# Sorted experts with a two-part operand, and a reordered end of the stick-breaking mixer

## What is computed

```python
def moe_swiglu(h, w_router, wg, wu, wd):          # layer 1 of the first block
    logits = (xt @ w_router).astype(jnp.float32)
    top_v, top_i = lax.top_k(logits, TOP_K)       # 2 of 8 experts for each token
    gates = jax.nn.softmax(top_v, axis=-1)
...
    for e in range(N_EXPERTS):                    # wg, wu: 1024x3584, wd: 3584x1024
        y = y + gate[:, e:e + 1] * swiglu(xt, wg[e], wu[e], wd[e])

def stick_breaking_attention(q, k, v):            # 8 heads, in both layers of the second block
    z = jnp.einsum('bqhd,bshd->bhqs', qb, k) * scale
    log_beta = jax.nn.log_sigmoid(z)
    log_1m = jnp.where(strict, jax.nn.log_sigmoid(-z), 0.0)
    after = lax.cumsum(log_1m, axis=3, reverse=True) - log_1m
    a = jnp.where(strict, jnp.exp(log_beta + after), 0.0)
    return jnp.einsum('bhqs,bshd->bqhd', a, v)
```

## Time and profile before

| | us |
|---|---|
| median of 3 runs | 2488.77 (2488.15 to 2489.57) |
| profiled execution, its own time | 2488.49 |
| its span, first to last instruction | 2486.8 |
| PE busy in the span | 2458.5 |
| DVE busy | 2083.3 |
| ACT busy | 1586.6 |

### The profile page before, as it was taken

The page is one execution under the profiler, slowest core; times in us unless marked ns, Lnnn a source line. Parts: engine busy times, 40 slices in busy tenths (PEclk is TensorE's granted clock), DMA queues, the critical chain, the costliest instruction groups (busy, mean ns, idle before and its releaser), DMA issues.

```text
span 2486.8 us, 44150 instructions
## 1 busy us (share of the span) xinstructions
PE 2458.5 (99%) x17270; PEld 2248.2 (90%) x17270; DVE 2083.3 (84%) x2832; ACT 1586.6 (64%) x2312; POOL 172.0 (7%) x244
## 2 busy tenths in 40 slices
PE   9999999999999999999999999999999999999999
PEld 9999998999999999999998899998899899988998
DVE  5688857999999999999999799786898798786665
ACT  5644556888888888888887644557544544566543
POOL 2111021000000000000000111010111011010000
PEclk9999999999999999999999999999999999999999
DMA  7698545999999999999999688433688587432642
GB/s 295 230 360 318 197 167 205 394 363 378 365 381 365 381 365 379 368 376 369 375 367 393 231 303 321 176 128 128 234 317 295 217 325 288 160 128 77 220 178 77
DMA packets 136637, 696.21 MB, mean 280 GB/s; under 512 B 16528, under 2 KB 16656, under 8 KB 87728
## 3 DMA queue, kind: packets, MB, share of 16 engines
q1 hardware_dynamic: 109872, 598.79, 64.5%
q0 software_dynamic: 23424, 88.16, 9.2%
q10 hardware_dynamic: 3136, 6.43, 0.7%
HBM read 683.28 MB, written 13.24 MB: 280 GB/s over the span
## 4 chain that ended last, share of the span: by engine, by line
PE 89%; DVE 6%; ACT 3%; issue 1%; POOL 0%; DVEq 0%; ACTq 0%; POOLq 0%
PE ps L2390 16%; PE ps L1985 15%; PE ps L1986 15%; PE ps L1987 15%; PE ps L2552 12%; PE ps L2392 8%; DVE w_parts L1705 1%; DVE w_parts L1325 1%; PE ps L2522 1%; PE ps L2014 1%; ACT w_parts L1113 1%; DVE a_parts L1713 1%; PE ps L2010 1%; PE ps L2221 0%; DVE xT L1347 0%
## 5 line engine op out<-in xcount | busy, mean ns | idle before, releaser
L2390 PE MATMUL ps<-a_parts,w_parts 128*128 128x512 f32 x1760 | 618.8, 393 | 1.6 <-DVE a_parts L1290 1.3
L1705 DVE TENSOR_TENSOR w_parts<-ring,w_parts 128x1024 fp32r<-128x1024 f32 x448 | 548.3, 1224 | 53.6 <-ACT w_parts L1113 51.7
L1985 PE MATMUL ps<-w_parts 128*112 128x256 f32 x1792 | 515.5, 288 | 0.0
L1987 PE MATMUL ps<-w_parts 128*112 128x256 f32 x1792 | 498.6, 278 | 0.0
L1986 PE MATMUL ps<-w_parts 128*112 128x256 f32 x1792 | 498.5, 278 | 0.0
L2392 PE MATMUL ps<-a_parts,w_parts 128*128 128x256 f32 x1760 | 492.5, 280 | 0.0
L1113 ACT ACTIVATE w_parts<-ring 128x1024 fp32r<-128x1024 f32 x448 | 472.0, 1054 | 0.0
L2390 PEld LDWEIGHTS ps<-a_parts,w_parts 128*128 128x128 f32 x1760 | 329.8, 187 | 75.7 <-issue 3.6
L2392 PEld LDWEIGHTS ps<-a_parts,w_parts 128*128 128x128 f32 x1760 | 332.3, 189 | 0.0
L1985 PEld LDWEIGHTS ps<-w_parts 128*112 128x112 f32 x1792 | 312.9, 175 | 11.8 <-issue 0.2
L1986 PEld LDWEIGHTS ps<-w_parts 128*112 128x112 f32 x1792 | 312.7, 174 | 11.7
(11 more groups left out here) (274 smaller groups left out, 4468.1 us busy)
## 6 DMA issues: line engine op xcount, KB each, us to landing
ring<-wstream SPq DMA_DIRECT2D x378, 1024.0 KB, 7.1
ring<-wstream SPq DMA_DIRECT2D x378, 512.0 KB, 5.8
proj<-astream POOLq DMA_DIRECT2D x144, 512.0 KB, 5.6
slot_rows<-branch POOLq DMA_DIRECT2D x7, 448.0 KB, 6.9
slot_out<-slot_rows POOLq DMA_DIRECT2D x1, 3136.0 KB, 14.6
sq<-slot_rows ACTq DMA_DIRECT2D x49, 64.0 KB, 5.4
slot_out<-pT ACTq DMA_DIRECT2D x49, 64.0 KB, 5.4
vtok<-crow POOLq DMA_DIRECT2D x3, 512.0 KB, 4.1
```

The costliest lines, as they stand in the source:

```text
L1705: nc.vector.tensor_tensor(up_lo[:, n % 2, at], ring[:, s, at], up_hi[:, n % 2, at], ALU.subtract)\
L1985: mm(o, stationary[0], moving[0], start=start, stop=False, skip_group_check=True)
L1987: return mm(o, stationary[1], moving[0], start=False, stop=stop, skip_group_check=True)
L2390: mm(ps[:, bank, :], hi, a_parts[:, :, k, :], start=k == 0, stop=k == KB - 1, skip_group_check=True)
```

## The change

It has two parts.

**Experts.** `router` counts also how many of the experts 1 to 6 have at most FEW = 64 tokens, and sets `wide` if these are fewer than three (five small DVE instructions in place of two). After chunk 1 of expert 0, `in_order` (six DVE instructions of 8 to 64 columns) ranks the experts by count, in descending order, with expert 0 kept first and expert 7 last. SP reads the order and loads the weights of positions 1 to 6 at addresses worked out at run time. At positions 4, 5 and 6 the hidden rows are at most 64: `hid_hi` is 64 columns, and the rest stands in columns 64 to 127 of the same stationary operand. Two products (against the weights' high part and rest) take the place of three, so `down` has 4 matmuls in place of 6. The result then lies in two row halves of PSUM; ACT copies the first (L1172's place), and DVE adds the second to it, in the first two chunks of the next expert. (The product rest x rest is computed as well.)

**Mixer.** The tails of pair 3 get banks 0 and 1, the products of pairs 1 and 2 get banks 4 and 5, so that `tails(3)` follows `tails(2)` at once and `weigh` waits less for copies. Seven of nine fills go. DVE and ACT take pair 3's steps earlier; `o_sum(3)` moves into the out-projection and one block moves ahead of `o_sum(4)`.

```diff
+FEW = 64
+FEW_AT = (4, 5, 6)
...
+        def after_banks(pair):
+            return ps[:, 0:2, 0:T + P] if pair == 3 else ps[:, 6:8, 0:T + P]
+        def weigh_bank(pair):
+            return ps[:, (3, 4, 5, 3)[pair], 0:T]
...
+            def tile(i, a, b):
+                at, c = divmod(i - STARTS[MOE_STAGE], FX)
+                if not 0 < at < NE - 1:
+                    return wstream[i, :, a:b]
+                if at not in first_tile:
+                    if at == 1:
+                        sp.wait_ge(order_ready, 1)
+                    first_tile[at] = nc.sync.value_load(order[0:1, at:at + 1], min_val=STARTS[MOE_STAGE],
+                                                        max_val=STARTS[MOE_STAGE] + (NE - 1) * FX)
+                return wstream[bass.ds(first_tile[at] + c, 1), :, a:b].rearrange("a p n -> p (a n)")
...
                 stick_exp(m, 1)
+                stick_exp(m, 2)
                 o_root(m, 1)
+                cat_hi(m, range(2))
+                stick_exp(m, 3)
                 copy_sticks(m, 1)
-                hi_half(out, 1, 0)
-                cat_hi(m, range(2))
-                stick_exp(m, 2)
                 copy_sticks(m, 2)
                 o_root(m, 2)
                 cat_hi(m, range(2, 4))
-                stick_exp(m, 3)
-                hi_half(out, 1, 1)
+                hi_half(out, 1, 0)
                 copy_sticks(m, 3)
                 for j in range(3, 6):
                     o_root(m, j)
                     cat_hi(m, [j + 1])
+                    if j == 3:
+                        hi_half(out, 1, 1)
...
-                        nc.scalar.activation(hid_hi[:, n % 2, 0:CAP], ps[:, 6, 0:CAP], ACT.Copy)\
-                            .then_inc(xhid_hi, 1)
+                        w = FEW if n_e in FEW_AT else CAP
+                        nc.scalar.activation(hid_hi[:, n % 2, 0:w], ps[:, 6, 0:w], ACT.Copy).then_inc(xhid_hi, 1)
...
+                softplus(3)
+                exponent(2)
+                beta(3)
                 cat_scaled(m, 0)
                 cat_scaled(m, 1)
-                exponent(2)
-                softplus(3)
-                beta(3)
+                exponent(3)
+                cat_rest(m, 0)
+                cat_rest(m, 1)
...
+                        if n_e in FEW_AT:
+                            rest, w = hid_hi[:, n % 2, FEW:2 * FEW], FEW
+                        else:
+                            rest, w = hid_lo[:, n % 2, 0:CAP], CAP
+                        nc.vector.tensor_tensor(rest, ps[:, 6, 0:w], hid_hi[:, n % 2, 0:w],
                                                 ALU.subtract).then_inc(xhid_lo, 1)
...
+                        if n_e - 1 in FEW_AT and c < 2:
+                            cols = slice(c * 512, (c + 1) * 512)
+                            dve.wait_ge(ye_top, 2 * FEW_AT.index(n_e - 1) + c + 1)
+                            nc.vector.tensor_tensor(ye[0:FEW, cols], ye[0:FEW, cols],
+                                                    ps[FEW:2 * FEW, 2 * ((n_e - 1) % 2) + c, :],
+                                                    ALU.add).then_inc(ye_ready, 1)
                         if n_e == 0 and c == 1:
+                            in_order(False)
                             slots()
...
-                    pe.wait_ge(zm_ready, 4 * (m - 1))
+                    pe.wait_ge(arg_ready, 4 * (m - 1))
                     blocks(0, 0)
+                    o_sum(m, 3)
+                    blocks(0, 1)
                     o_sum(m, 4)
-                    blocks(0, 1)
                     blocks(0, 2)
+                    blocks(0, 3)
                     o_sum(m, 5)
-                    blocks(0, 3)
...
                 o_sum(m, 1)
-                pe.wait_ge(zm_ready, 4 * (m - 1))
-                fill(5, 3)
                 tails(m, 2)
+                tails(m, 3)
                 weigh(m, 1)
                 o_sum(m, 2)
-                fill(5, 3)
-                tails(m, 3)
                 weigh(m, 2)
-                o_sum(m, 3)
-                fill(5, 3)
+                fill(7, 2)
                 weigh(m, 3)
                 outproj1(m)
...
+                    if n // FX in FEW_AT:
+                        rows, products = 2 * FEW, ((hid_hi, wd_hi), (hid_hi, wd_lo))
+                    else:
+                        rows, products = CAP, ((hid_hi, wd_hi), (hid_hi, wd_lo), (hid_lo, wd_hi))
+                    for i, (h, w) in enumerate(products):
                         for half in range(2):
+                            ins = mm(ps[0:rows, bank + half, :], h[:, b, 0:rows], w[:, b, half * D // 2:(half + 1) * D // 2],
+                                     start=c == 0 and i == 0, stop=c == FX - 1 and i == len(products) - 1,
+                                     skip_group_check=True)
```

More of the change, by code:

```diff
@@ L94 @@
                ("lmult0", P), ("lmult1", T), ("strict", T + P), ("barred", T + P), ("cos", T), ("sin", T),
-               ("invcnt", 4 * 16), ("iota", NE), ("slots", CAP)):
+               ("invcnt", 4 * 16), ("iota", NE), ("slots", CAP), ("tie", NE)):
     CONST[_n] = (_at, _w)
@@ L191, in build @@
         slot_of = ctx.enter_context(nc.sbuf_tensor("slot_of", [P, 2, TT], mybir.dt.int32))
+        order = ctx.enter_context(nc.sbuf_tensor("order", [P, NE], mybir.dt.int32))
+        ranks = sb("ranks", [P, 3, NE])
+        versus = sb("versus", [P, NE, NE])
         slot_rows = nc.dram_tensor("slot_rows", (NE * CAP, D), fp32).ap()
@@ L525, in load @@
                 if up:
-                    sp.dma_start(ring[:, s, 0:UP], wstream[i, :, 0:UP]).then_inc(tile_in[s], 16)
+                    sp.dma_start(ring[:, s, 0:UP], tile(i, 0, UP)).then_inc(tile_in[s], 16)
                 if down:
-                    sp.dma_start(ring[:, s, UP:TILE], wstream[i, :, UP:TILE]).then_inc(down_in[s], 16)
+                    sp.dma_start(ring[:, s, UP:TILE], tile(i, UP, TILE)).then_inc(down_in[s], 16)
             def up_free(i):
@@ L1604, in mixer2 @@
                 lo_outproj(m, 1, 0)
[L1605 to L1608, removed]
+                for k in range(4, KB):
                     cat_scaled(m, k)
+                    if k == 5:
+                        lo_outproj(m, 1, 1)
                     cat_rest(m, k)
@@ L1716, in moe_wide @@
             def moe_wide():
+                in_order(True)
                 slots()
@@ L1888, in router @@
                         .then_inc(place_ready, 1)
-                after(dve, "dve", nc.vector.tensor_reduce(m1[:, 0, :], ps[:, 7, TT * NE:(TT + 1) * NE], AX, ALU.max))
-                nc.vector.tensor_scalar(wide[:, :], m1[:, 0, :], CAP + 0.5, None, ALU.is_gt)\
-                    .then_inc(wide_ready, 1)
+                count = ps[:, 7, TT * NE:(TT + 1) * NE]
+                after(dve, "dve", nc.vector.scalar_tensor_tensor(
+                    versus[:, 0, 1:NE - 1], count[:, 1:NE - 1], FEW + 0.5, ones[:, 1:NE - 1], ALU.is_le, ALU.mult,
+                    accum_out=ranks[:, 2, 0:1]))
+                after(dve, "dve", nc.vector.tensor_reduce(m1[:, 0, :], count, AX, ALU.max))
+                after(dve, "dve", nc.vector.scalar_tensor_tensor(
+                    ranks[:, 0, :], count, float(NE), C("tie"), ALU.mult, ALU.add))
+                after(dve, "dve", nc.vector.tensor_scalar(ranks[:, 2, 1:2], ranks[:, 2, 0:1], len(FEW_AT) - 0.5, None,
+                                                          ALU.is_lt))
+                nc.vector.scalar_tensor_tensor(wide[:, :], m1[:, 0, :], CAP + 0.5, ranks[:, 2, 1:2],
+                                               ALU.is_gt, ALU.max).then_inc(wide_ready, 1)
                 up_lo_half(1, 0, 0)
@@ L2549, in down @@
                     pe.wait_ge(tile_used, r * FX + (STARTS[MOE_STAGE] + n + 1))
-                    for i, (h, w) in enumerate(((hid_hi, wd_hi), (hid_hi, wd_lo), (hid_lo, wd_hi))):
+                    if n // FX in FEW_AT:
[3 more added lines that the diff above has]
+                    for i, (h, w) in enumerate(products):
                         for half in range(2):
-                            ins = mm(ps[0:CAP, bank + half, :], h[:, b, 0:CAP], w[:, b, half * D // 2:(half + 1) * D // 2],
-                                     start=c == 0 and i == 0, stop=c == FX - 1 and i == 2, skip_group_check=True)
+                            ins = mm(ps[0:rows, bank + half, :], h[:, b, 0:rows], w[:, b, half * D // 2:(half + 1) * D // 2],
+                                     start=c == 0 and i == 0, stop=c == FX - 1 and i == len(products) - 1,
+                                     skip_group_check=True)
                     ins.then_inc(xdown_done, 1)
```

50 lines of the change are left out of this document (32 added, 18 removed).

## The result

The changed kernel takes 2464.76 us (median of 4 runs, 2463.47 to 2465.22), the kernel before 2488.72 (2488.15 to 2489.57) beside it. The ratio is 0.9902, 95% interval 0.9891 to 0.9914: 24.0 us less, where 23.8 had been forecast. That the sum fits so well says little about its terms: four of them were off, and their errors cancel. The profiled execution has a span of 2462.4 us, 24.4 less than before.

A forecast was written before the change was run, and what follows sets the result against it. PE was taken to set the pace, with a second chain through ACT and DVE as long. Gains and costs, 27.3 - 3.0 - 1.2 - 1.3 + 2.0 = 23.8 us, gave 2465 us, range 2459 to 2471.

The forecast's parts named there:

- pace of 84 short chunks: Short experts: two of six down products removed, pace 4.264 to 3.94 us a chunk, 27.3 us gained.
- additions: DVE after each short expert: two PSUM additions, six in all, charged 0.5 us each, 3.0 us lost.
- less slack for the token split: DVE's two L1755 per expert sit in reduced slack: 0.2 us more for each of six, 1.2 us lost.
- router, addresses: Three more DVE instructions in the router and SP's run-time load addresses: both hidden, costing nothing.
- two mixers: Before the out-projection: block of nine products moved ahead of `o_sum(4)`, 1.0 us a mixer, 2.0 gained in all.
- The loop over two chunks: Short experts: waits through ACT, DVE and PE close in 7.76 us per two chunks; 3.94 a chunk with 0.055 left over.
- PE keeps the bound: Rival, short experts: PE still sets the pace, 3.80 us a chunk, gain 38.6, total 2454 us; chance 0.15.
- DMA full: Rival, expert stage: DMA already full, pace stays 4.26, only added work shows, 2491 us; chance 0.08.
- DMA in part: Rival, short experts: DMA holds only 390 GB/s, pace 4.12, gain 12, total 2480 us; chance 0.15.
- The clock: Rival, mixers: PE's clock falls to 1.2 GHz behind waits up to 2.5 us, 14 us lost, 2479; chance 0.03.
- SP's addresses: Rival, positions 1 to 6: slow address work makes SP slowest, 57 us more at 2.0 us a load, about 2546; chance 0.03.
- The wide path: Rival, experts: each chunk runs 24 full-float32 products, over 1000 us more; chance under 0.01.

The follow-up runs named there:

- sort alone: Kernel before plus descending expert order and weight loads at run-time addresses, no short form, old mixer: 2491.24 us, ratio 1.0006.
- Half the bytes: Changed kernel, but SP loads only half the columns of each weight tile in the short experts: 2464.44 us, one run.
- the shorter split: Changed kernel, but in short experts ACT and DVE make only 512 of 1024 columns of the up weights' second half: 2459.47 us, one run.
- the fifth product: Changed kernel with one down product made twice in each chunk of the short experts: 2476.51 us, one run.
- the rest first: Changed kernel, but in short experts DVE makes the rest of the hidden rows before that of the next down weights: 2457.65 us, ratio 0.9876.

## Why the prediction was right, and where it wasn't

| term | predicted | measured | from |
|---|---|---|---|
| pace of 84 short chunks | 27.3 | 23.9 | 4.264 - 3.98 |
| additions | -3.0 | -3.4 | chunks 1 and 2 against pace |
| less slack for the token split | -1.2 | 0 | 1.34 to 1.59 over pace, 1.36 to 1.54 before |
| `in_order` | -1.3 | -1.3 | sort alone |
| router, addresses | 0 | 0 | sort alone |
| two mixers | 2.0 | 4.6 | table above |
| sum | 23.8 | 23.8 | 24.0 by the medians |

**The pace: mechanism right, size off by 0.04.** The loop over two chunks was named ahead of the run. Half the bytes rules out DMA as the bound, the shorter split the sum of DVE's or ACT's work, the fifth product PE's own work, and taking one step out of the loop brought the pace down to what PE needs. One link was named wrong: DVE's rest of the first half of the up weights stands between ACT's first high part and the rest of the down weights, where the prediction had ACT's high part of the down weights; the two take about the same time, which is luck. ACT's stretch to the product came out at 3.64 to 3.67 for 3.64. What was mis-sized is the way back through PE: the prediction has 0.92 for the products, 2.99 for the next up, 0.21 to ACT's next high part and 0.11 left over, 4.23; the shorter-split kernel shows 4.35. The four products take 0.99 us to the next up product when they have waited (970.14 to 971.13), and 0.93 in the kernel with the rest first, in which they have not. 0.12 over two chunks is 0.06; the changed kernel, at 3.98, shows 0.04. The 0.11 left over has no reason in this loop: it is what PE had beside its products in the kernel before, and without it the sum is 3.88.

**PE keeps the bound, 2454: wrong.** Weight loads wait 0.145 us a chunk. PE's own pace would have been 3.85 and not 3.80. **DMA full, 2491: wrong.** 396 GB/s were moved. **DMA in part, 2480: wrong here**, but it is the next limit, as the kernel with the rest first showed. **The clock, 2479: did not occur**: the longest wait there is 0.46 us, not 2.5. Where a wait of 2.14 us was made, the fall came and cost 1.4 and 2.3 us a mixer, not the 7 feared. **SP's addresses: wrong**, by the sort alone. **The wide path did not run.**

**The additions** took 690 ns each (0.65 predicted from the nearest row). They cost 1.25, 1.25 and 0.9 us after the three short experts, each time over two chunks and less what these took over the pace before. The token split cost nothing more than before: it was priced for lost slack, but it sits in chunks that were beyond the pace already (by 1.36 to 1.54 us in an expert), so there was no slack to lose.

**The router** grew by three instructions and DVE's wait ahead of L1784 fell from 1.38 to 0.77 us: hidden, as said.

**The mixer: the step failed.** That ACT's longer path "lets `o_sum(2)` go at about 1713.0" rests on a wait for pair 1's squares that the code does not have. `o_sum(2)` came 1.9 us earlier than that, and `o_sum(4)`, of which the prediction had said that it should start "at the same distance from the mixer's first fill as today", 2.1 us earlier. With the wait in place the mixers give back 2.3 and 3.5 us, of which 0.9 and 1.2 are the wait, so the assumed step does cost about what the prediction charged, and a fall of the clock besides. The total hit 24 by luck, because this error (+2.6) and the split's (+1.2) stood against the pace's (-3.4) and the additions' (-0.4).

Experts 1 to 3 and 7 kept their pace (4.26 to 4.31 in chunks 4 to 19), as claimed.

What stays open: the 2 us ahead of the mixers in the kernel with the added wait, seen once; why ACT was late once behind the expert stage with five products; and whether a longer ring, or gathers spread over the expert, would hold 3.85 through it, which was not tried.

## What to carry to other kernels

When an engine's work is cut, walk the loop of waits through the other engines and note over how many chunks it closes: that loop, not the next busiest engine, gave the new pace to 1% (to 2.5% without the left-over added to it). The same loop tells the next edit: moving one 1.1 us operation of DVE behind the handoff was worth 7 us in the short experts and 16 in all, two thirds of the original change again. When the limits stand this close, ask the windows in pieces: a mean of 407 GB/s hid one stretch at 371 that did all the harm. And read the count in each wait from the code before building a timeline on it.

## What the runs showed of the hardware

A DMA busy share of 0.99 at 375 GB/s was not full: 396 ran at 1.01 and 416 at 1.02. But in the stretches with the gathers 371 ran at 1.02 too, while ACT waited for loads. So the share doesn't tell the rate. With the weight loads alone DMA held 416 GB/s over 42 us, close to the 417 and 418 of the short catching-up stretches.

PE's granted clock fell to 0.50 behind one wait of 2.14 us in each mixer of the kernel with the added wait, and behind one of 1.80 us in the kernel with five products; it stayed full behind one of 1.57 us in the kernel before and behind 0.46 in the changed one. The page doesn't show this: such a fall is shorter than one of its 40 slices, so the windows have to be asked. DVE operations of 128 x 1024 recorded at 1.22 us follow each other at 1.13 to 1.14 us.
